# Moving four modulation columns and the last bias into the borders between stages

## The reference, cut to what matters

```
c_act = silu(c)
mod = c_act @ w_ada[l] + b_ada[l]                    # 1024 -> 6 x 1024
sh1, sc1, g1, sh2, sc2, g2 = split(mod, 6)
h = rmsnorm(x, norm_gains[l, 0]) * (1.0 + sc1) + sh1
y = token_mixer(h, ...)                              # in2, attention, out2
x = x + g1 * rmsnorm(y, norm_gains[l, 1])
h = rmsnorm(x, norm_gains[l, 2]) * (1.0 + sc2) + sh2
y = square(relu(h @ w1[l] + b1[l])) @ w2[l] + b2[l]
x = x + g2 * rmsnorm(y, norm_gains[l, 3])
```

## Time and profile before

| | |
|---|---|
| median of 3 runs | 1186.43 us (1185.67 to 1188.95) |
| the profiled execution's own time | 1188.14 us |
| its span, from the first to the last instruction | 1186.3 us |
| PE busy | 1098.8 us, 93% of the span |
| DVE busy | 726.3 us, 61% |
| ACT busy | 517.5 us, 44% |
| POOL busy | 133.6 us, 11% |
| mean granted TensorE clock | 0.951 of full |

### The profile page before, as it was taken

The page is one execution under the profiler, slowest core; times in us unless marked ns, Lnnn a source line. Parts: engine busy times, 40 slices in busy tenths (PEclk is TensorE's granted clock), DMA queues, the critical chain, the costliest instruction groups (busy, mean ns, idle before and its releaser), DMA issues.

```text
span 1186.3 us, 16936 instructions
## 1 busy us (share of the span) xinstructions
PE 1098.8 (93%) x7036; PEld 970.3 (82%) x7036; DVE 726.3 (61%) x1004; ACT 517.5 (44%) x736; POOL 133.6 (11%) x151
## 2 busy tenths in 40 slices
PE   5998899988999999888889899999979997999998
PEld 4798899866999988676667799998769866999885
DVE  3476875576766575746674676666664556666343
ACT  3453242244444443424663444343255656555331
POOL 1004663114000000510000400000110000000000
PEclk9897899989899999888999899999989999999999
DMA  9332002124887777253783587767534332665540
GB/s 293 106 121 75 1 1 72 63 85 137 297 275 224 252 271 278 71 180 132 115 209 107 177 282 256 253 236 281 184 106 143 107 93 85 184 191 196 189 166 36
DMA packets 113581, 193.67 MB, mean 163 GB/s; under 512 B 4674, under 2 KB 85073, under 8 KB 113378
## 3 DMA queue, kind: packets, MB, share of 16 engines
q1 hardware_dynamic: 109842, 179.66, 45.2%
q0 software_dynamic: 3248, 11.83, 4.5%
q10 hardware_dynamic: 416, 1.11, 0.2%
HBM read 188.39 MB, written 4.19 MB: 162 GB/s over the span
## 4 chain that ended last, share of the span: by engine, by line
PE 82%; DVE 8%; ACT 5%; issue 2%; SPq 1%; DMA 1%; POOL 1%; DVEq 0%; ACTq 0%; POOLq 0%
PE ps L415 22%; PE ps L417 22%; PE ps L416 22%; PE ps L1971 2%; PE ps L1956 2%; PE ps L1185 2%; PE ps L1949 1%; PE ps L1195 1%; PE ps L1422 1%; PE ps L1129 1%; DVE ARR L399 1%; DVE XL L551 1%; ACT ARR L386 1%; PE ps L481 1%; DMA ring<-in_ffn_w_gate_up_dram 1%
## 5 line engine op out<-in xcount | busy, mean ns | idle before, releaser
L399 DVE TENSOR_TENSOR ARR<-ring,ARR 128x2048 fp32r<-128x2048 f32 (+1 forms) x143 | 321.2, 2251 | 209.7 <-ACT ARR L386 209.7
L415 PE MATMUL ps<-XH,ARR 128*128 128x256 f32 x1232 | 354.6, 288 | 15.4 <-DVE XL L551 8.7
L386 ACT ACTIVATE ARR<-ring 128x2048 fp32r<-128x2048 f32 (+1 forms) x143 | 267.0, 1874 | 204.8 <-PE ps L417 149.6
L416 PE MATMUL ps<-XL,ARR 128*128 128x256 f32 x1232 | 351.6, 285 | 0.0
L417 PE MATMUL ps<-XH,ARR 128*128 128x256 f32 x1232 | 351.4, 285 | 0.0
L415 PEld LDWEIGHTS ps<-XH,ARR 128*128 128x128 f32 x1232 | 238.1, 193 | 20.7 <-issue 16.9
L416 PEld LDWEIGHTS ps<-XL,ARR 128*128 128x128 f32 x1232 | 238.1, 193 | 0.1
L417 PEld LDWEIGHTS ps<-XH,ARR 128*128 128x128 f32 x1232 | 238.0, 193 | 0.0
L415 PE MATMUL ps<-ARR 128*128 128x512 f32 x420 | 171.0, 407 | 8.9 <-DVE ARR L503 4.6
L416 PE MATMUL ps<-ARR 128*128 128x512 f32 x420 | 167.5, 399 | 0.0
L417 PE MATMUL ps<-ARR 128*128 128x512 f32 x420 | 167.4, 399 | 0.0
(11 more groups left out here) (343 smaller groups left out, 1278.9 us busy)
## 6 DMA issues: line engine op xcount, KB each, us to landing
ring<-in_ffn_w_gate_up_dram SPq DMA_DIRECT2D x44, 1024.0 KB, 5.9
ring<-in_w_dram SPq DMA_DIRECT2D x32, 1024.0 KB, 5.2
ring<-in_w_ada_dram SPq DMA_DIRECT2D x24, 1024.0 KB, 5.3
ring<-in_ffn_w_down_dram SPq DMA_DIRECT2D x22, 1024.0 KB, 5.0
ring<-in_even_w_in_dram SPq DMA_DIRECT2D x13, 1024.0 KB, 5.6
ring<-in_w_in_dram SPq DMA_DIRECT2D x9, 1024.0 KB, 5.3
ring<-in_mla_w_q_b_dram SPq DMA_DIRECT2D x6, 768.0 KB, 6.7
ring<-in_even_w_out_dram SPq DMA_DIRECT2D x4, 1024.0 KB, 4.8
```

Of the source, the lines that this page charges most:

```text
L386: e.activation(split(i)[0], raw(i), ACT.Copy).then_inc(*up("hi", ("hi", i)))
L399: e.tensor_tensor(lo, raw(i), hi.bitcast(F32), ALU.subtract).then_inc(*up("lo", ("lo", i), ("raw free", i)))
L415: e.matmul(out, lhs[0], rhs[0], start=first, stop=False)
L416: e.matmul(out, lhs[0], rhs[1], start=False, stop=False)
```

## The change

The four columns 1, 2, 4 and 5 leave `down`. Columns 1 and 2 go to norm 1: PE does column 1 between the transposes of t=0 and of t=1, and column 2 after those of t=1; DVE does its part of both after its part of the norm (`dve_norm(e, 1, ...)`), ahead of the MLA stage. Columns 4 and 5 go on PE between the end of `down` of layer 1 and the transposes of `m0`, and on DVE after `dve_scaled` of `m0`, ahead of `dve_in2`. A gate's `GN` is multiplied in earlier (`dve_gate_gain`, ahead of the piece at `k0` = 18): once into the accumulator `ACCA`, once into the bias row `G12`, each over 1024 columns; after the sum over partitions only the addition is left. The bias of `w2` goes ahead of the transposes of `m1` (`pe_last_bias`): it opens the four sums, in banks 0, 1, 6 and 7, and until the end only the four banks 2 to 5 are dealt in turn, to the transposes of `m1` and to `w1`. Two waits of POOL ahead of the loads of the MLA stage (`pool_mla_start`) keep them behind columns 1 and 2, and the waits for the columns are moved to where each is read.

```diff
@@ -169,11 +169,11 @@
 
 
     def __init__(self, aps):
-        self.aps, self.held, self.place, self.turn, self.n = aps, {}, {}, 0, 8
+        self.aps, self.held, self.place, self.turn, self.first, self.n = aps, {}, {}, 0, 0, 8
 
     def take(self, use):
 
-        i = self.turn % self.n
+        i = self.first + self.turn % self.n
         self.turn += 1
         before = self.held.get(i)
         self.held[i], self.place[use] = use, i
@@ -189,7 +189,7 @@
         return self.aps[self.place[use]]
 
     def second(self):
-        self.held, self.place, self.turn, self.n = {}, {}, 0, 8
+        self.held, self.place, self.turn, self.first, self.n = {}, {}, 0, 0, 8
 
 
 def program(nc, a):
@@ -434,13 +434,14 @@
         def parts_of(n):
             return [(o, min(512, n - o)) for o in range(0, n, 512)]
 
-        def pe_rows(e, tag, kc, n, xT, xready, bias=None, between=None, tail=1):
+        def pe_rows(e, tag, kc, n, xT, xready, begun=False, between=None, tail=1):
+
 
             parts = parts_of(n)
             before = {}
             for t in range(2):
                 for j in range(len(parts)):
-                    before[t, j] = banks.take((tag, t, j))
+                    before[t, j] = None if begun else banks.take((tag, t, j))
             per = max(1, 2048 // n)
             firsts = list(range(0, kc, per))
             head, last = firsts[:len(firsts) - tail], firsts[len(firsts) - tail:]
@@ -460,18 +461,18 @@
                         if (t, j) == (0, 0) and (c == k0 or c % 2 == 0):
                             e.wait_ge(*at(xready(c // 2)))
                         k = mm3(e, b, cut(xT, ALL, c, slice(t * P, t * P + P)),
-                                cut(hilo, ALL, c - k0, slice(o, o + m)), c == 0, c == kc - 1 and bias is None)
-                    if k1 == kc and bias is not None:
-                        k = e.matmul(b, ones1, bias[0:1, o:o + m], start=False, stop=True)
+                                cut(hilo, ALL, c - k0, slice(o, o + m)), c == 0 and not begun, c == kc - 1)
                     here = [("full", (tag, t, j))] if k1 == kc else []
                     if (t, j) == (1, len(parts) - 1):
                         here.append(("used", w))
                     if here:
                         k.then_inc(*up("products", *here))
 
-        def pe_transposed(e, tag, src, c_n, ready):
+        def pe_transposed(e, tag, src, c_n, ready, between=None):
             before = [banks.take((tag, c)) for c in range(c_n // 2)]
             for t in range(2):
+                if t and between:
+                    between(e)
                 for step in ready(t):
                     e.wait_ge(*at(step))
                 for c in range(c_n):
@@ -638,7 +639,10 @@
             return [("x", i, 0), ("x", i, 1)]
 
         def pe_norm(e, i):
-            pe_transposed(e, f"n{i}", XN, 8, xn_ready(i))
+
+            pe_transposed(e, f"n{i}", XN, 8, xn_ready(i), (lambda e: pe_modulation_column(e, 1)) if i == 1 else None)
+            if i == 1:
+                pe_modulation_column(e, 2)
 
         def act_norm(e, i, tf_before):
             act_scaled(e, f"n{i}", XT, ln_scale(i), ln_shift(i), [xt_free[f"n{i}"]], tf_before)
@@ -1622,7 +1626,7 @@
             if j in (2, 5):
                 for o in (0, 512):
                     b = bank(e, ("mod", j, o))
-                    e.wait_ge(*at(("ada", j)))
+                    e.wait_ge(*at(("gain in", j)))
                     e.matmul(b, cst("ones"), acc[:, o:o + 512], start=True, stop=True).then_inc(
                         *up("gates", ("full", ("mod", j, o)), *([("summed", j)] if o else [])))
                 return
@@ -1632,18 +1636,23 @@
                 k = e.matmul(b[:, i:i + 1], acc[:, i * P:i * P + P], one_col, start=True, stop=True)
             k.then_inc(*up("gates", ("full", ("mod", j, 0)), ("summed", j)))
 
+        def dve_gate_gain(e, j):
+
+            g, acc = G12[:, j // 3, :], ACCA[:, j % 2, :]
+            e.wait_ge(*at(("gate rows", j // 3)))
+            e.wait_ge(*now("ada"))
+            e.tensor_tensor(acc, acc, GN, ALU.mult).then_inc(*up("ada", ("gain in", j)))
+            e.tensor_tensor(g, g, GN, ALU.mult).then_inc(*up("ada"))
+
         def dve_modulation_column(e, j):
             if j in (2, 5):
                 g = G12[:, j // 3, :]
                 for o in (0, 512):
                     use = ("mod", j, o)
                     e.wait_ge(*at(("full", use)))
-                    if o == 0:
-                        e.wait_ge(*at(("gate rows", j // 3)))
-                    e.tensor_tensor(g[:, o:o + 512], ps(use), g[:, o:o + 512], ALU.add).then_inc(*up("ada", ("free", use)))
                     e.wait_ge(*now("ada"))
-                    e.tensor_tensor(g[:, o:o + 512], g[:, o:o + 512], GN[:, o:o + 512], ALU.mult).then_inc(
-                        *up("ada", ("gate", j // 3, o)))
+                    e.tensor_tensor(g[:, o:o + 512], ps(use), g[:, o:o + 512], ALU.add).then_inc(
+                        *up("ada", ("free", use), ("gate", j // 3, o)))
                 return
             use = ("mod", j, 0)
             e.wait_ge(*at(("full", use)))
@@ -1681,8 +1690,7 @@
                                     cut(XT, ALL, c), c == 0, c == 7)
                     k.then_inc(*up("products", ("used", w), ("full", tag)))
             pe_rows(e, ("down", layer), 22, 1024, HT, lambda c: ("ht", layer, 2 * c),
-                    between={6: lambda e: pe_modulation_column(e, 3 * layer + 1),
-                             20: lambda e: pe_modulation_column(e, 3 * layer + 2)}, tail=2)
+                    tail=2)
             pe_norm(e, i) if i < 3 else None
 
         def act_ffn(e, layer, i):
@@ -1724,8 +1732,8 @@
                 e.wait_ge(*at(("h first", layer, j)))
                 e.tensor_tensor(lo, u, hi.bitcast(F32), ALU.subtract).then_inc(*up("swiglu", ("ht", layer, j)))
             for k0 in range(0, 22, 2):
-                if k0 in (6, 20):
-                    dve_modulation_column(e, 3 * layer + (1 if k0 == 6 else 2))
+                if k0 == 18:
+                    dve_gate_gain(e, 3 * layer + 2)
                 dve_split(e, ahead(("down", layer), k0, k0 < 20))
             if layer == 0:
                 dve_residuals(e, ("down", layer), i, x_after(i - 1), place_of["min", 0])
@@ -1758,6 +1766,8 @@
             for step in x_after(1):
                 e.wait_ge(*at(step))
             e.wait_ge(*at(("used", place_of[("down", 0), 20])))
+            e.wait_ge(*at(("summed", 1)))
+            e.wait_ge(*at(("summed", 2)))
             e.dma_start(MK, a["mla_mask"]).then_inc(*up("odd", by=16))
             e.dma_start(FR, a["rope_freq"]).then_inc(*up("odd", "odd", by=16))
             e.dma_start(PI_, a["positions"].rearrange("b (t p) -> p (b t)", p=P), allow_slow_non_contiguous=True
@@ -2219,7 +2229,7 @@
         def mod_shift(k):
             return lambda c: MOD[:, 24 * k + c:24 * k + c + 1]
 
-        mods = [("mod in", j) for j in (0, 1, 3, 4)]
+        mods = [("mod in", j) for j in (0, 1)]
 
 
         carve = Carve(0)
@@ -2455,10 +2465,18 @@
                 e.wait_ge(*at(("h2 first", i)))
                 e.tensor_tensor(lo, x, hi.bitcast(F32), ALU.subtract).then_inc(*up("squared", ("ht2", i)))
 
+        def pe_last_bias(e):
+
+            e.wait_ge(*at("b2"))
+            for n, i in enumerate((0, 1, 6, 7)):
+                t, j = n // 2, n % 2
+                b = bank(e, ("w2", t, j), i)
+                e.matmul(b, ones1, BT2[0:1, 512 * j:512 * j + 512], start=True, stop=False)
+            banks.first, banks.n = 2, 4
+
         def pe_w1_w2(e):
             pe_columns(e, "w1", 32, XT, xt_step("m1"))
-            e.wait_ge(*at("b2"))
-            pe_rows(e, "w2", 32, 1024, HT2, lambda c: ("ht2", 2 * c), bias=BT2, tail=3)
+            pe_rows(e, "w2", 32, 1024, HT2, lambda c: ("ht2", 2 * c), begun=True, tail=3)
 
         def split_rest(split_, e, tag, kc, per):
             for k0 in range(0, kc, per):
@@ -2498,10 +2516,13 @@
             pe_mout_rest(e)
             pe_norm(e, 2)
             pe_ffn(e, 1, 3)
+            pe_modulation_column(e, 4)
+            pe_modulation_column(e, 5)
             pe_transposed(e, "m0", XN, 8, m_ready(0))
             pe_in2(e)
             pe_attend(e, SWA, pe_beside_heads)
             pe_out2_rest(e)
+            pe_last_bias(e)
             pe_transposed(e, "m1", XN, 8, m_ready(1))
             pe_w1_w2(e)
 
@@ -2542,7 +2563,7 @@
             act_attend(e, SWA, act_beside_heads)
             e.activation(SM[:, 6:7], one_col, ACT.Sqrt).then_inc(*up("rms"))
             act_gated(e, "out2", 0)
-            act_scaled(e, "m1", XT, mod_scale(1), mod_shift(1), [xt_free["m1"]], ("xt", ("m0", 3)))
+            act_scaled(e, "m1", XT, mod_scale(1), mod_shift(1), [xt_free["m1"], ("mod in", 3), ("mod in", 4)], ("xt", ("m0", 3)))
             act_w1(e)
             split_rest(act_split, e, "w2", 32, 2)
             act_gated(e, "w2", 1)
@@ -2568,6 +2589,8 @@
```

(7 more changed lines are left out.)

## The result

The changed kernel takes 1178.59 us (median of 7 runs, 1174.68 to 1183.97), the kernel before 1186.43 (7 runs, 1183.70 to 1193.12) on the same chip. The ratio is 0.9925, interval 0.9896 to 0.9954: 8.9 us off, with an interval from 5.5 to 12.3 (the two medians themselves lie 7.8 apart). The forecast was 11.4 off, 1175.0, with a range from 1171.5 to 1180.0.

A forecast was written before the change was run, and what follows sets the result against it. PE was taken to bound `down`, with idle time in the borders. Terms 7.0 + 4.7 + 0.6 + 0.6 - 1.2 - 0.3 = 11.4 us off the median 1186.43 gave 1175.0 us, range 1171.5 to 1180.

The forecast's parts named there:

- `down` is bound by PE: In `down`, PE sets the pace, so moving two columns out saves 3.50 us in each layer, 7.0 us off.
- POOL's 0.6: Border of `m0`: without the columns DVE and POOL's rows are done sooner, so ACT starts earlier; 0.6 us off.
- the removed time isn't seen: Rival, `down` and `w2`: splits or weights set the pace and PE only idles where work was; 1186, chance 0.03.
- The gate gains at nothing: In `down`, the two early `GN` multiplications, at most 1.36 us each, fit DVE's 3.29 us idle time; cost 0.
- Norm 1: Norm 1's border: columns fit PE's idle time, 0 to 0.2 over, but DVE's part delays `min`'s second piece; 1.2 us on.
- a wait far over 1.3: Sign of being wrong: PE's wait for DVE at `min`'s second piece far over 1.3 us; about 1 was expected.
- the first of the rivals: Rival, `min`: the clock falls again behind PE's new wait for DVE, losing 2.2 us; 1177.2, chance 0.12.
- The border of `m0` and `va2`: Columns 4 and 5 fit PE's 8.19 us idle at cost 0; their DVE parts delay `va2`, 0.3 us on.
- The bias: End of `w2`: three biases leave the stream (3.66 us) and ACT starts 1.05 us sooner; 4.7 us off.
- that rival: Rival, `w1`: four banks in place of eight make pairs wait for ACT; 1193 at 1.5 us each, chance 0.03.
- The clock in `m1`'s border: Border of `m1`: with PE's idle time filled by the bias, the transposes run at a quicker clock; 0.6 us off.

The follow-up runs named there:

- DVE late: Changed kernel with DVE's part of columns 1 and 2 put behind the splits of `min`'s second and third pieces: 1174.86 us, ratio 0.9891.
- 128 rows: Changed kernel with the four last-bias matmuls using all 128 rows of the array in place of one, same sums: 1176.72 us, ratio 0.9899.
- two later studies: The unaltered changed kernel timed twice more against the kernel before: 1176.95 us, ratio 0.9906, and 1175.77 us, ratio 0.9899.
- Both and filled: Changed kernel, DVE's columns 1 and 2 behind `min`'s splits, bias matmuls on 128 rows, column 5's matmuls done three times in `m0`'s border: 1174.61 us, 0.9881.

## Why the prediction was right

**`down` is bound by PE: right.** Six products with a column between them cost the column's time and no more came in its place. From column 0's matmuls to the first transposes of norm 1 it was 112.08 us and is 108.82 in the first profile of the change, 3.3 for the 3.50 forecast. Layer 1 carries its 3.50 and POOL's 0.6 together: gu1 to m0 is 205.1 and 205.6 without, 200.5 to 202.0 with the columns moved, 4.4 by the means against 4.1. The rival that the removed time isn't seen falls with this.

**The gate gains at nothing: right.** They took 1.22 each, below the bound of 1.36, and ended 1.04 us before DVE was wanted.

**Norm 1: right up to min2, and what lies behind it missed.** The wait at min2 came where it was put, released by DVE L399, and costs 0.6 to 0.9 (1.2 was taken). DVE late shows it to be the queue's order. On PE the columns were to be 0 to 0.2 over; from the first transposes to `min` it is 7.1 to 7.8 with them and 6.6, 7.3 and 7.8 without, which is 0 to 0.5. Together, from the first transposes to min2, it is 15.9 to 16.0 for a mean of 14.8: 1.2, as taken. But PE stands idle there for 2.1 to 3.0 us, and the forecast had about 1 and named a wait far over 1.3 as a sign that it is wrong. That sign came. The sum survives it because PE is sooner at the piece than it was thought to be, 5.8 to 6.2 us behind the start of `min` for 7.7 before; the idle time's other price is the clock behind it, the first of the rivals, which was given 0.12. It came about in all three profiled executions of the changed kernel, at 1.55 us (7.25 for 5.70), and not in the two other kernels with the same order.

**The border of `m0` and `va2`: right.** Both columns fit. `va2` takes 13.2 to 14.1, mean 13.7, with the columns' DVE parts ahead of it, and 12.8 and 13.8 without: 0.4 for the 0.3, but not told apart by two executions.

**The bias: 0.3 too high.** w2 is 3.36 shorter (92.73 to 89.37) and ACT's start 1.05 nearer, 4.4 for 4.7. The 1.22 for each in the stream was 1.12; its own duration was nearer than the distance less the products. It fits in the border, where `out2` to `m1` stays at 4.75 (in all executions but DVE late's), and four banks cost `w1` nothing (92.4 with either), so that rival is refuted.

**The clock in `m1`'s border: the term that failed.** It was put at 0.6 and is nothing: 5.1 to 5.3 from m1 to w1 where it was 5.3. The working took it that PE's idle time had its price and that the bias would remove it; the bias removed the idle time and not the fall. With 128 rows it is 0.86.

The terms so corrected: 2.0 for layer 0, 4.4 for layer 1, 4.4 for the bias, less 0.4, are 10.4, and 8.9 where the clock falls behind the wait. The three studies gave 8.9, 11.2 and 12.0, and the spans of the change's three profiled executions are 9.6, 9.1 and 9.4 under that of the one before. That the forecast's 11.4 lies so near the two later studies is in part luck: the 0.6 for the clock in `m1`'s border and the 0.3 of the bias weren't there, and the fall behind the wait had been left to a rival.

The first profile has a loss of its own. From N0 to the first transposes of norm 1 it is 1.2 to 1.7 us behind the four others in its order: PE stood idle for 1.29 at 332.55, behind a transfer for which ACT had waited 4.78 us,

```profile
328.16 1.92 ACT L386 ACTIVATE ARR<-ring 128x2048 fp32r<-128x2048 f32 x1 [4.78 <-DMA ring<-in_ffn_w_gate_up_dram]
```

where before it waited 2.49. Of the ten other kernels' and repeats' traces only one has idle time of PE there, 0.23, so it isn't put down to the change. Its longer wait at min2 is no second loss, since PE came sooner to it: from the first transposes to min2 it takes 15.9 us, the four others 16.0. Whether the median of 1178.59 in the first study is owed to such a loss can't be said from one profile. In the two later studies the profiled execution was the longest of the changed kernel's (1179.12 and 1178.78, with medians of 1176.95 and 1175.77); whether the others had the fall behind the wait no trace tells.

What stays open: whether any version beats the changed kernel. Both and filled has the lowest ratio, 0.9881 (0.9858 to 0.9904), but the intervals of the changed kernel's three (0.9925, 0.9906, 0.9899) all overlap with that one. Its stages say 1.1 for DVE's order up to min2 (and 0.4 up to gu1, or 3 to 4 where that spares the fall), 0.9 for the bias rows less what `w1` takes back (nothing, 0.5, 0.5 and 2.1), and 0.5 for the filling.

## What to carry to other kernels

Work of a stream that the bounding engine runs without a gap is worth its full distance when it is moved to where that engine waits, whatever little it is; but follow each of its consumers too. Here the main price was four small instructions of DVE, 1.86 us, that stood ahead of a split which PE needed next: PE's wait for it cost 0.6 to 0.9 us, and the clock that fell behind the wait 1.55 more in three of five executions. Put such consumers behind the next thing that the bounding engine waits for. And don't count on a better clock for having filled a gap: read it at the border and in the stage behind it, since a fall avoided in the one was found in the other in three of four executions.

## What the runs showed of the hardware

Four matmuls of one row by 512 columns, 3.70 us of them right ahead of the transposes, left the granted clock at 0.83 in the border and the transposes at 3.53; with 128 rows, 3.60 us of them gave 1.00 and two groups of 1.09. This was seen in all four kernels with 128 rows (4.40 from m1 to w1) and not in any of the six executions with one row there (5.1 to 5.3).

The clock's falls move. Held through norm 1 in one execution, it fell behind the wait that followed (0.54). Held in the border of `m1` in four, it fell at the start of `w1` in three (0.59 over 8.3 us in one, 0.57 over 3.7 us in two), which took 2.1, 0.5 and 0.5 us.

A wait of PE of the same kind may or may not be followed by a fall: with 2.15, 2.28 and 2.99 us of it the next 24 matmuls took 7.25 us, with 2.07 and 2.08 they took 5.70. Behind it the same work took 26.5 us at a grant of 0.92 and 29.8 at 0.81.
